# Experts of a hybrid block: the down product as seven half-sized products in place of eight, with the weight sums and three of the low parts on GpSimd

## The chip, the cores and the metric

The kernel runs on one core of a Trainium2 chip. The metric is the device time of one execution in microseconds. Each 32-bit product is made of three TensorE passes in a reduced format (fp32r): a value is split into a high part (a rounded copy) and a low part (value minus high part), and low·high, high·low and high·high are added up in PSUM.

## The reference

The block is a hybrid mixer (RWKV-7 and gated linear attention), a short convolution mixer, and a mixture of experts at the end. Only the last is touched:

```
def expert_choice_ffn(h, w_router, w_gate, w_up, w_down):
    aff = softmax(h @ w_router)                          # 2048 tokens, 16 experts
    g, idx = top_k(swapaxes(aff, 1, 2), cap)             # cap = 256 tokens per expert
    xs = h[idx]                                          # [16, 256, 1024]
    hid = silu(einsum('becd,edf->becf', xs, w_gate)) * einsum('becd,edf->becf', xs, w_up)
    ys = einsum('becf,efd->becd', hid, w_down) * g[..., None]
    return scatter_add(ys, idx)                          # [2048, 1024]
```

Each of the three weight matrices of an expert is 1024x1024 in float32 (4 MB), so an expert reads 12 MB.

## The kernel before, in words

Everything before the last stage is left as it is. The last stage (`experts`, with `choose` and `Choice`) loops over the 16 experts; each engine runs its own in-order program and they meet through counting semaphores.

- **Weights.** An expert's weights come in 12 pieces of 128x2048 (1 MB): pieces 0 to 7 are alternately gate and up (256 output columns each), 8 to 11 are two blocks of 128 rows of the down matrix each. SyncE loads a piece into one of four buffers (`w_loaded`) as soon as the low part of the piece four back is made (`load`, L2873). ScalarE makes the high part (`split_hi`, L2885), VectorE the low part (`split_lo`, L2889), each in a ring of six buffers.
- **Gate and up, f = 0 to 7.** For each of eight blocks of 128 hidden columns TensorE makes 24 gate and 24 up matmuls of 256 columns. ScalarE takes silu, VectorE multiplies (`hidden`), ScalarE makes its high part and VectorE its low part. f may start only when the `hidden` of f - 2 is made. After each odd f two more pieces are split. Beside f = 0 to 3 VectorE also marks the next expert's tokens (`mark`, 16 instructions), and before the `hidden` of f = 4 it reads their list out of PSUM (`keep`); GpSimd waits for that, and then gathers them by two indirect DMAs.
- **Turn.** 16 transposes of the gathered tokens of the next expert, once the `hidden` of f = 6 and 7 are made; ScalarE and VectorE make `x_hi`, `x_lo` (four instructions each).
- **Down.** 8 blocks of hidden rows x 2 halves of the tokens x 2 halves of the columns x 3 passes = 96 matmuls of 512 columns, into banks 4 to 7. Beside it ScalarE and VectorE split four pieces of the next expert.
- **End.** Four VectorE instructions scale the result (L3123), and GpSimd adds it to the output by two indirect DMAs.

GpSimd does no arithmetic on large tiles in this stage; in the first stage it does (L1150).

Of the kernel before, what the change touches and what calls it, by code (L numbers as in the profile page):

```python
# [14 lines left out]
F32 = mybir.dt.float32  # L15
# [2819 lines left out]
def experts(nc, k, wg, wu, wd, aff, idx_all, gate_all, out):  # L2835
# [8 lines left out]
    CH, LOADED, SPLIT, W = 12, 4, 6, KD * 256  # L2844
    F32R = mybir.dt.float32r
    with Phase("ex") as ctx:
        s = semaphores(nc, ctx, ["row", "load0", "load1", "load2", "load3", "hi", "lo", "used", "turned", "x_hi", "x_lo", "gu", "silu",
                                 "hid", "hid_hi", "hid_lo", "y", "ys", "idx", "gates", "consts", "parts", "at", "now", "hot", "listed", "chosen", "gate", "first"])
# [3 lines left out]
        raw = sb(nc, ctx, "w_loaded", [P, LOADED, W])  # L2852
        w_hi = [sb(nc, ctx, f"w_hi{i}", [P, W], F32R) for i in range(SPLIT)]
# [4 lines left out]
        h_hi = sb(nc, ctx, "hid_hi", [P, KD, CAP], F32R)  # L2858
        h_lo = sb(nc, ctx, "hid_lo", [P, KD, CAP], F32R)
        sl = sb(nc, ctx, "silu", [P, 2, CAP])  # L2860
        hid = sb(nc, ctx, "hidden", [P, 2, CAP])
# [8 lines left out]
        made = Choice(nc, ctx, k, s, idx_all, gate_all)  # L2870

        def load(sp, e, c):

            views = (gv, uv) if c < CH else (gv[1:], uv[1:])
            c = c % CH
            dst = raw[:, c % LOADED, :]
            if c < 8:
                src = views[c % 2][e, :, :, (c // 2) * 256:(c // 2 + 1) * 256]
                dst = dst.rearrange("p (kb f) -> p kb f", f=256)
            else:  # L2880
                dst = dst.rearrange("p (kb d) -> p kb d", d=D)
                src = dv[:, bass.ds(e * KD + (c - 8) * 2, 2), :]
            sp.dma_start(dst, src).then_inc(loads[c % LOADED], 16)

        def split_hi(act, e, c):  # L2885
            act.wait_ge(loads[c % LOADED], e * 48 + 16 * (c // LOADED + 1))
            nc.scalar.activation(w_hi[c % SPLIT][:], raw[:, c % LOADED, :], ACT.Copy).then_inc(s["hi"], 1)  # L2887

        def split_lo(dve, e, c):  # L2889
            dve.wait_ge(s["hi"], e * CH + c + 1)  # L2890
            nc.vector.tensor_tensor(w_lo[c % SPLIT][:], raw[:, c % LOADED, :], w_hi[c % SPLIT][:].bitcast(F32), ALU.subtract).then_inc(s["lo"], 1)  # L2891

        def passes(psum, lh, ll, rh, rl, first, last):

            nc.tensor.matmul(psum, ll, rh, start=first, stop=False)  # L2895
            nc.tensor.matmul(psum, lh, rl, start=False, stop=False)  # L2896
            return nc.tensor.matmul(psum, lh, rh, start=False, stop=last)  # L2897
# [31 lines left out]
        choose(nc, k, aff, made, xg, sl, Beside())  # L2929
        with nc.Block() as block:  # L2930
            @block.sync
            def _(sp):
                def turn(e, last, c0=0):
                    for c in range(c0, CH - LOADED if last else CH):
                        sp.wait_ge(s["lo"], e * CH + c + 1)
                        load(sp, e, c + LOADED)
                turn(0, False)
                with sp.Fori(1, NE - 1) as e:
# [4 lines left out]
            def _(pool):  # L2943
# [14 lines left out]
                def scatter(e, copied):  # L2958
# [8 lines left out]
                    for h in range(2):  # L2967
                        pool.wait_ge(sent[h], e * 16 + 16)
                gather(0, 1)
                pool.wait_ge(s["idx"], 2)  # L2970
                nc.gpsimd.tensor_tensor(mark[:], k.ident[:, 0:1], k.ident[:, 0:1], ALU.mult).then_inc(s["first"], 1)
                pool.wait_ge(s["first"], 1)
                with pool.Fori(0, NE - 1) as e:
                    for h in range(2):
                        pool.wait_ge(gathered[h], e * 16 + 16)
                    pool.wait_ge(s["turned"], e * 4 + 4)
                    gather(e + 1, e * 4 + 3)
                    scatter(e, e * 4 + 5)
                scatter(NE - 1, NE * 4 - 1)

            @block.tensor
            def _(pe):
# [8 lines left out]
                def turn(e, last):  # L2991
                    pe.wait_ge(s["x_lo"], e * 4 + 4)
                    for f in range(KD):
# [6 lines left out]
                        for half in range(2):  # L3000
                            c = 2 * q + half
                            if f % 2 == 0:
                                pe.wait_ge(s["lo"], e * CH + c + 1)
# [13 lines left out]
                    for f in range(KD):  # L3017
                        c = 8 + f // 2
                        pe.wait_ge(s["hid_lo"], e * KD + f + 1)
                        if f % 2 == 0:  # L3020
                            pe.wait_ge(s["lo"], e * CH + c + 1)
                        for h in range(2):
                            hs = slice(h * P, (h + 1) * P)
                            for b in range(2):
                                o = (f % 2) * D + b * 512
                                mm = passes(bank[4 + 2 * h + b][:], h_hi[:, f, hs], h_lo[:, f, hs], w_hi[c % SPLIT][:, o:o + 512],
                                            w_lo[c % SPLIT][:, o:o + 512], f == 0, f == KD - 1)
                        if f % 2:
                            mm.then_inc(s["y"], 1)
# [5 lines left out]
            def _(act):  # L3035
# [217 lines left out]
```

## Time and profile before

| what | us |
|---|---|
| median of 3 runs (lowest, highest) | 3490.54 (3489.82, 3493.35) |
| profiled execution: time | 3489.02 |
| profiled execution: span | 3487.2 |
| TensorE matmuls busy | 3289.8 |
| VectorE busy | 2187.5 |
| ScalarE busy | 1461.8 |
| GpSimd busy | 563.4 |

Busy times are sums over an engine's instructions. In timelines a row may merge several like instructions (xN); its time then runs from the first one's start to the last one's end. One instruction alone lasts a little longer than the distance at which the next can follow. The experts take the span from about 2330 us on.

### The profile page before, as it was taken

To read this page: it belongs to the slowest core of one execution; us is meant where nothing else is said; L and a number is where in the kernel's file an instruction comes from. 1 tells how busy PE (TensorE), PEld (TensorE's weight loads), DVE (VectorE), ACT (ScalarE), POOL (GpSimd) and SP (SyncE) were. 2 spreads that over 40 slices of the span, in tenths; PEclk is the share of its full clock that TensorE was granted. 3 is DMA by queue.
4 is the path that set the end of the run, shared out by engine and by line. 5 is a ranking of instruction groups with operands and counts; after the bars stand their busy time and mean duration, and the time that the engine had idled before them with its cause. 6 is when DMAs were issued, how large, how long until landed. Compare 5 with 4: busy or idle time off the path is not lost. (4 is left out here: it accounts for less than half of the span.)

```text
span 3487.2 us, 75240 instructions
## 1 busy us (share of the span) xinstructions
PE 3289.8 (94%) x31246; PEld 2817.5 (81%) x31246; DVE 2187.5 (63%) x3703; ACT 1461.8 (42%) x2121; POOL 563.4 (16%) x792
## 2 busy tenths in 40 slices
PE   7999999999699998989989999959999999999997
PEld 5778878788577886867877878749999999999997
DVE  4666766667554655677787866676555656565563
ACT  5445444444255665332233224424444444444442
POOL 3555555555100000000000000000100110011000
PEclk9999999999999999989999999959999999999999
DMA  4221222211233434422122244446666666666662
GB/s 146 57 83 52 66 75 61 80 51 51 67 127 109 142 113 156 134 85 68 65 73 85 77 157 157 148 137 203 214 209 207 212 205 206 214 199 215 200 217 73
DMA packets 361839, 452.83 MB, mean 130 GB/s; under 512 B 15189, under 2 KB 300149, under 8 KB 361589
## 3 DMA queue, kind: packets, MB, share of 16 engines
q1 hardware_dynamic: 350200, 407.33, 36.0%
q0 software_dynamic: 9216, 33.56, 4.1%
q10 hardware_dynamic: 2176, 8.39, 0.6%
q8 instruction: 188, 3.08, 0.4%
q14 instruction: 59, 0.48, 0.0%
HBM read 382.10 MB, written 67.13 MB: 129 GB/s over the span
## 5 line engine op out<-in xcount | busy, mean ns | idle before, releaser
L2895 PE MATMUL bank<-ex_x_hi,ex_w_lo 128*128 128x256 f32 x2048 | 581.4, 284 | 2.0 <-DVE ex_x_lo L3077 2.0
L2896 PE MATMUL bank<-ex_x_lo,ex_w_hi 128*128 128x256 f32 x2048 | 580.2, 283 | 0.0
L2897 PE MATMUL bank<-ex_x_hi,ex_w_hi 128*128 128x256 f32 x2048 | 580.1, 283 | 0.0
L2891 DVE TENSOR_TENSOR ex_w_lo<-ex_w_loaded,ex_w_hi 128x2048 fp32r<-128x2048 f32 x192 | 433.8, 2289 | 226.7 <-ACT ex_w_hi L2887 222.3
L2887 ACT ACTIVATE ex_w_hi<-ex_w_loaded 128x2048 fp32r<-128x2048 f32 x192 | 359.4, 1904 | 171.7 <-PE bank L2897 169.3
L2895 PEld LDWEIGHTS bank<-ex_x_hi,ex_w_lo 128*128 128x128 f32 x2048 | 393.6, 192 | 2.8 <-issue 2.2
L2896 PEld LDWEIGHTS bank<-ex_x_lo,ex_w_hi 128*128 128x128 f32 x2048 | 393.6, 192 | 0.6
L2897 PEld LDWEIGHTS bank<-ex_x_hi,ex_w_hi 128*128 128x128 f32 x2048 | 393.7, 192 | 0.0
L2338 PE MATMUL bank<-sc_tokens_hi,sc_w_lo 128*128 128x512 f32 x672 | 266.9, 397 | 28.6 <-DVE hidden_hT_split L2468 12.5
L2951 POOL CAST ex_idx<-kept_masks 128x2 uint32 (+1 forms) x16 | 3.0, 186 | 1735.7 <-POOLq L79 1424.7
L2340 PE MATMUL bank<-sc_tokens_hi,sc_w_hi 128*128 128x512 f32 x672 | 264.6, 394 | 0.0
L264 PE MATMUL bank<-columns_columns_hi,weights_weights_lo 128*128 128x512 f32 x544 | 226.6, 417 | 9.9 <-DVE columns_columns_lo L849 4.4
L3051 ACT ACTIVATE ex_hid_hi<-ex_hidden 128x256 fp32r<-128x256 f32 x128 | 53.4, 417 | 415.8 <-DVE ex_hidden L3100 415.8
L760 ACT ACTIVATE rw_E<-bank 128x256 f32<-128x256 f32 x160 | 61.0, 381 | 377.2 <-PE bank L371 377.2
L266 PE MATMUL bank<-columns_columns_hi,weights_weights_hi 128*128 128x512 f32 x544 | 214.0, 393 | 0.0
L265 PE MATMUL bank<-columns_columns_lo,weights_weights_hi 128*128 128x512 f32 x544 | 213.8, 393 | 0.0
L2895 PE MATMUL bank<-ex_w_hi,ex_hid_lo 128*128 128x512 f32 x512 | 200.8, 392 | 0.0
L2897 PE MATMUL bank<-ex_w_hi,ex_hid_hi 128*128 128x512 f32 x512 | 199.4, 390 | 0.0
L2896 PE MATMUL bank<-ex_w_lo,ex_hid_hi 128*128 128x512 f32 x512 | 199.2, 389 | 0.0
L1150 POOL TENSOR_TENSOR weights_weights_lo<-plain_weights,weights_weights_hi 128x1024 fp32r<-128x1024 f32 x67 | 164.1, 2450 | 205.8 <-ACT weights_weights_hi L614 205.6
L2338 PEld LDWEIGHTS bank<-sc_tokens_hi,sc_w_lo 128*128 128x128 f32 x672 | 128.2, 191 | 61.1 <-DVE hidden_hT_split L2468 14.3
L3100 DVE TENSOR_TENSOR ex_hidden<-ex_silu,bank 128x256 f32<-128x256 f32 x128 | 53.5, 418 | 157.1 <-PE bank L2897 157.1
(498 smaller groups left out, 8303.2 us busy)
## 6 DMA issues: line engine op xcount, KB each, us to landing
ex_w_loaded<-in_wg SPq DMA_DIRECT2D x64, 1024.0 KB, 5.4
ex_w_loaded<-in_wu SPq DMA_DIRECT2D x64, 1024.0 KB, 6.2
ex_w_loaded<-in_wd SPq DMA_DIRECT2D x64, 1024.0 KB, 5.1
plain_weights<-in_w_in SPq DMA_DIRECT2D x70, 512.0 KB, 4.7
gl_ada_tile<-in_ada_w SPq DMA_DIRECT2D x48, 512.0 KB, 4.4
plain_first_w<-in_sc_w_in SPq DMA_DIRECT2D x24, 1024.0 KB, 5.2
plain_columns<-hT_dram SPq DMA_DIRECT2D x14, 1024.0 KB, 7.5
plain_columns<-in_x SPq DMA_DIRECT2D x16, 512.0 KB, 5.7
```

The source lines that it names most:

```text
L264: nc.tensor.matmul(psum, lo[:, kb, :], h_hi[:, :, at], start=(kb == 0), stop=False)
L265: nc.tensor.matmul(psum, hi[:, kb, :], h_lo[:, :, at], start=False, stop=False)
L266: mm = nc.tensor.matmul(psum, hi[:, kb, :], h_hi[:, :, at], start=False, stop=(kb == KD - 1))
L760: nc.scalar.activation(eb[:], k.psum[:].rearrange("p (i x) -> p i x", x=512)[:, 4:6, 256:384].rearrange("p i (j t) -> p i j t", t=C), ACT. ...
L1150: nc.gpsimd.tensor_tensor(w_lo[n % 3], wraw[n % 3], w_hi[n % 3].bitcast(F32), ALU.subtract).then_inc(s["w_lo"], 1)
L2338: nc.tensor.matmul(psum, w_lo[:, at, kb, :], hi[:, kb, :], start=(kb == 0 and not more), stop=False, skip_group_check=more)
L2340: mm = nc.tensor.matmul(psum, w_hi[:, at, kb, :], hi[:, kb, :], start=False, stop=(kb == H - 1), skip_group_check=more)
L2887: nc.scalar.activation(w_hi[c % SPLIT][:], raw[:, c % LOADED, :], ACT.Copy).then_inc(s["hi"], 1)
L2891: nc.vector.tensor_tensor(w_lo[c % SPLIT][:], raw[:, c % LOADED, :], w_hi[c % SPLIT][:].bitcast(F32), ALU.subtract).then_inc(s["lo"], 1)
L2895: nc.tensor.matmul(psum, ll, rh, start=first, stop=False)
L2896: nc.tensor.matmul(psum, lh, rl, start=False, stop=False)
L2897: return nc.tensor.matmul(psum, lh, rh, start=False, stop=last)
```

## The change

The down product `hid @ w_down` of an expert is cut into 2x2 blocks on each side: A11, A12, A21, A22 are `hidden` by halves of the tokens and of the hidden rows (stored turned), B11 to B22 the down matrix by halves of its rows and columns. Seven products replace eight (Winograd's form):

- S3 = A11 - A21, S2 = A22 - S3, S1 = A21 + A22, S4 = A12 - S2, made on VectorE; T1 = B12 - B11, T2 = B22 - T1, T3 = T2 - B11, T4 = B21 - T2, made on GpSimd (`block_sum`).
- The products, in the order in which TensorE makes them, are A11·B11, S3·T3, S1·T1, S2·T2, A12·B21, A22·T4, S4·B22: below P0 to P6. Each is 4 x 3 matmuls of 512 columns, 84 in all. P4, P5 and P6 go on adding in the banks of P0, P1 and P2.
- VectorE adds the banks up: `middle` 1 is u2 = P0 + P3, 2 is v2 = u2 + P1, 3 is v2 + P2. P5 may start only after `middle` 2 and P6 after `middle` 3, as they write the same banks.

There are now 15 pieces to split per expert (8, and B11, T3, T1, T2, B21, T4, B22 as numbers 8 to 14) in rings of five. The low parts of pieces 0, 1 and B21 are made on GpSimd, the other 12 on VectorE. The high and low parts of the hidden blocks are made in 7 instructions of 512 columns each, in place of 8 of 256 each. The down matrix is loaded by blocks: no bytes are added. The core of the diff:

```diff
-    CH, LOADED, SPLIT, W = 12, 4, 6, KD * 256
+    CH, LOADED, PIECES, SPLIT, W, H = 12, 4, 15, 5, KD * 256, KD // 2
+    B11, T3, T1, T2, B21, T4, B22 = range(8, 15)
+    POOL_LO = (0, 1, B21)
...
+                def block_sum(e, c):
+                    n = SUMS.index(c)
+                    for slot in {T1: (0, 1), T2: (2,), T3: (), T4: (3,)}[c]:
+                        pool.wait_ge(loads[slot], e * 48 + 48)
...
+                    if c == T3:
+                        lo_made(pool, e, B11)
...
+                    nc.gpsimd.tensor_tensor(raw_of(c), one, other, ALU.subtract).then_inc(s["t"], 1)
...
+                def turn(e, last):          # GpSimd
+                    block_sum(e, T1)
+                    block_sum(e, T2)
+                    if not last:
...
+                        gather(e + 1, e * 4 + 3)
+                    block_sum(e, T3)
+                    block_sum(e, T4)
+                    split_lo(pool, nc.gpsimd, e, B21, s["lo_pool"])
+                    if not last:
+                        split_lo(pool, nc.gpsimd, e + 1, 0, s["lo_pool"])
+                        split_lo(pool, nc.gpsimd, e + 1, 1, s["lo_pool"])
...
+                    for n, a in enumerate(A_ORDER):          # TensorE
+                        c, more = B11 + n, n >= 4
+                        pe.wait_ge(s["a_lo"], e * 7 + LO_ORDER.index(a) + 1)
+                        lo_made(pe, e, c)
+                        if a == A12:
+                            pe.wait_ge(s["p1"], e + 1)
+                        if a in (A22, S4):
+                            pe.wait_ge(s["middle"], e * 3 + (2 if a == A22 else 3))
+                        for kb in range(H):
...
                     for f in range(KD):                      # ScalarE
...
+                        if f == 3:
+                            hidden_hi(e, A11)
+                            hidden_hi(e, S3)
+                        if f == 7:
+                            hidden_hi(e, S1)
                         if f % 2:
+                            act.wait_ge(s["gu"], e * 2 * KD + 2 * f + 2)
+                            split_hi(act, e, f + 4)
+                            if f == 7:
+                                hidden_hi(e, S2)
+                                hidden_hi(e, A12)
+                            split_hi(act, e, f + 5)
+                    hidden_hi(e, A22)
+                    act.wait_ge(s["y"], e * 7 + 1)
+                    act.wait_ge(s["idx"], e * 4 + 3)
+                    nc.scalar.activation(u2, bank[4][:], ACT.Copy).then_inc(s["p1"], 1)
+                    split_hi(act, e, T4)
+                    hidden_hi(e, S4)
                     if not last:
...                                                           # the four x_hi
+                    act.wait_ge(s["y"], e * 7 + 2)
+                    split_hi(act, e, B22)
+                    if not last:
+                        for d in range(SPLIT):
+                            act.wait_ge(s["y"], e * 7 + d + 3)
+                            split_hi(act, e + 1, d)
...
+                        if f == 3:                           # VectorE
+                            hidden_sum(e, S3)
+                            hidden_lo(e, A11)
+                        if f % 2 and f < 7:
+                            lo(f + 4)
+                            lo(f + 5)
+                    hidden_sum(e, S2)
+                    hidden_sum(e, S1)
+                    hidden_lo(e, S3)
+                    hidden_lo(e, S1)
+                    hidden_sum(e, S4)
+                    hidden_lo(e, S2)
+                    lo(T2)
+                    hidden_lo(e, A12)
+                    hidden_lo(e, A22)
+                    lo(T4)
+                    hidden_lo(e, S4)
+                    lo(B22)
+                    nc.vector.tensor_copy(gates[:], gav[...]).then_inc(s["gates"], 1)
...
+                    nc.vector.tensor_tensor(u2, u2, bank[5][:], ALU.add).then_inc(s["middle"], 1)
...
+                    nc.vector.tensor_tensor(v2, u2, bank[6][:], ALU.add).then_inc(s["middle"], 1)
...
+                    nc.vector.tensor_tensor(v2, v2, bank[7][:], ALU.add).then_inc(s["middle"], 1)
...
+                    scaled(1, 1, v2)
...                                                           # x_lo, two more sums, three more scaled
+                    if not last:
+                        for d in range(2, SPLIT):
+                            split_lo(dve, nc.vector, e + 1, d, s["lo"])
```

## Rows read from the trace of the kernel before

**Rows 1.** Windows, stage and one cycle: length; busy (xinstructions) PE, PEld, DVE, ACT, POOL; clock; DMA share, GB/s.
```profile
2330.00:3470.00 1140.00, 1135.29 (x8432) 1071.95 (x8432) 670.37 (x891) 490.05 (x523) 96.42 (x126) 1.00 0.64 202
...
2766.00:2836.50 70.50, 70.50 (x530) 66.67 (x529) 42.21 (x57) 31.15 (x33) 6.13 (x8) 1.00 0.66 208
```

**Rows 2.** Timeline, VectorE: start us, us, engine, line, what. `keep` of two experts in turn.
```profile
2443.80 0.16 DVE L2822 TENSOR_REDUCE kept_masks<-bank 128x4 f32 x1
...
2514.31 0.15 DVE L2822 TENSOR_REDUCE kept_masks<-bank 128x4 f32 x1
```

**Rows 3.** Timeline, TensorE: gate and up, turn, down, and the next expert's first matmul.
```profile
2812.76 0.28 PE L2897 MATMUL bank<-ex_x_hi,ex_w_hi 128*128 128x256 f32 x1
2812.89 1.91 PE L2906 MATMUL bank<-kept_masks,ex_x_gathered 128*128 128x128 f32 x16
2814.55 0.47 PE L2895 MATMUL bank<-ex_w_hi,ex_hid_lo 128*128 128x512 f32 x1
...
2836.21 0.39 PE L2897 MATMUL bank<-ex_w_hi,ex_hid_hi 128*128 128x512 f32 x1
2836.44 0.28 PE L2895 MATMUL bank<-ex_x_hi,ex_w_lo 128*128 128x256 f32 x1
```

**Rows 4.** Timeline, ScalarE: two high parts in a row, one alone, four of 512 columns.
```profile
2813.96 3.70 ACT L2887 ACTIVATE ex_w_hi<-ex_w_loaded 128x2048 fp32r<-128x2048 f32 x2
2817.56 2.04 ACT L3037 ACTIVATE ex_x_hi<-bank 128x512 fp32r<-128x512 f32 x4
2820.32 1.92 ACT L2887 ACTIVATE ex_w_hi<-ex_w_loaded 128x2048 fp32r<-128x2048 f32 x1 [0.72 <-PE bank L2897]
```

**Rows 5.** Timeline, VectorE, beside Rows 4 and the end of the down product.
```profile
2813.17 0.42 DVE L3100 TENSOR_TENSOR ex_hidden<-ex_silu,bank 128x256 f32<-128x256 f32 x1 [3.07 <-PE bank L2897]
...
2815.89 4.49 DVE L2891 TENSOR_TENSOR ex_w_lo<-ex_w_loaded,ex_w_hi 128x2048 fp32r<-128x2048 f32 x2 [1.38 <-ACT ex_w_hi L2887]
2820.30 2.48 DVE L3077 TENSOR_TENSOR ex_x_lo<-bank,ex_x_hi 128x512 fp32r<-128x512 f32 x4
...
2841.17 2.73 DVE L3123 SCALAR_TENSOR_TENSOR ex_y<-bank,ex_gates,ex_g_row 128x512 f32<-128x512 f32 x4 [0.21 <-DVE ex_gates L3116]
```

**Rows 6.** Groups, GpSimd, whole span: count, busy us, mean ns, idle before.
```profile
L1150 POOL TENSOR_TENSOR weights_weights_lo<-plain_weights,weights_weights_hi 128x1024 fp32r<-128x1024 f32 x67 | 164.1, 2450 | 205.8 <-ACT weights_weights_hi L614 205.6
L1155 POOL TENSOR_TENSOR rw_tanh_g_or_cs_before<-rw_cs,rw_sw 128x512 f32<-128x512 f32 x16 | 20.6, 1284 | 90.8 <-DVE rw_cs L881 90.8
```

**Rows 7.** Timelines, first stage: VectorE with both inputs in SBUF beside GpSimd.
```profile
133.19 3.27 DVE L849 TENSOR_TENSOR columns_columns_lo<-plain_columns,columns_columns_hi 128x1024 fp32r<-128x1024 f32 x1
...
132.57 2.81 POOL L1150 TENSOR_TENSOR weights_weights_lo<-plain_weights,weights_weights_hi 128x1024 fp32r<-128x1024 f32 x1
135.33 1.40 POOL L1161 TENSOR_TENSOR rw_nt<-rw_scores,mixers_masks 128x128 f32<-128x128 f32 x1
```

**Rows 8.** Timelines, first stage: VectorE with an input in PSUM beside GpSimd.
```profile
17.73 0.69 DVE L840 TENSOR_TENSOR plain_columns<-bank,rw_norm_cols 128x512 f32<-128x512 f32 x1 [0.42 <-PE bank L247]
...
16.99 2.35 POOL L1150 TENSOR_TENSOR weights_weights_lo<-plain_weights,weights_weights_hi 128x1024 fp32r<-128x1024 f32 x1 [16.53 <-ACT weights_weights_hi L614]
```

**Rows 9.** By line, VectorE: ns min/median/max of 16, first and last start.
```profile
L849 DVE TENSOR_TENSOR columns_columns_lo<-plain_columns,columns_columns_hi x16: 1217/1320/3273, 19.4 to 652.7; 128x1024 fp32r<-128x1024 f32 x16
L888 DVE TENSOR_SCALAR rw_a<-rw_a,rw_derived x16: 545/2472/2481, 54.6 to 839.6; 128x512 f32<-128x512 f32 x16
```

**Rows 10.** Transfers in window 2780 to 2851: count, KB each, median us to landing.
```profile
ex_w_loaded<-in_wd SPq DMA_DIRECT2D x4, 1024.0 KB, 5.3
...
ex_w_loaded<-in_wu SPq DMA_DIRECT2D x4, 1024.0 KB, 5.6
```

**Rows 11.** Timeline, GpSimd: the gather of the next expert's tokens.
```profile
2796.69 0.18 POOL L2951 CAST ex_idx<-kept_masks 128x2 uint32 x1 [19.34 <-DVE kept_masks L2822]
...
2799.02 0.96 POOL L2955 DMA_INDIRECT ex_x_gathered<-h_dram,ex_idx  x1 [0.30 <-issue]
```

More of the change, by code:

```diff
@@ L2843, in experts @@
     dv = wd.rearrange("o e (kb p) d -> p (o e kb) d", p=P)
-    CH, LOADED, SPLIT, W = 12, 4, 6, KD * 256
+    CH, LOADED, PIECES, SPLIT, W, H = 12, 4, 15, 5, KD * 256, KD // 2
     F32R = mybir.dt.float32r
+    B11, T3, T1, T2, B21, T4, B22 = range(8, 15)
+    A11, S3, S1, S2, A12, A22, S4 = range(7)
+    SUMS = (T1, T2, T3, T4)
+    LOAD_OF = {B11: 8, B22: 10, B21: 11}
+    BLOCK = {8: (0, 0), 9: (0, 1), 10: (1, 1), 11: (1, 0)}
+    BANK_OF = (4, 6, 7, 5, 4, 6, 7)
+    POOL_LO = (0, 1, B21)
+    DVE_LO = tuple(c for c in range(PIECES) if c not in POOL_LO)
+    POOL_STEP = CH // len(POOL_LO)
+    A_ORDER = (A11, S3, S1, S2, A12, A22, S4)
+    LO_ORDER = (A11, S3, S1, S2, A12, A22, S4)
+    HI_SLOT = (0, 1, 2, 3, 4, 5, 0)
     with Phase("ex") as ctx:
-        s = semaphores(nc, ctx, ["row", "load0", "load1", "load2", "load3", "hi", "lo", "used", "turned", "x_hi", "x_lo", "gu", "silu",
-                                 "hid", "hid_hi", "hid_lo", "y", "ys", "idx", "gates", "consts", "parts", "at", "now", "hot", "listed", "chosen", "gate", "first"])
+        s = semaphores(nc, ctx, ["row", "load0", "load1", "load2", "load3", "hi", "lo", "lo_pool", "t", "turned", "x_hi", "x_lo", "gu", "silu",
+                                 "hid", "a_sum", "a_hi", "a_lo", "y", "p1", "middle", "sum", "ys", "idx", "gates", "consts", "parts", "at", "now", "hot", "listed", "chosen", "gate", "first"])
         gathered = [ctx.enter_context(nc.semaphore(f"gathered{h}")) for h in range(2)]
@@ L2932, in _ @@
             def _(sp):
-                def turn(e, last, c0=0):
-                    for c in range(c0, CH - LOADED if last else CH):
-                        sp.wait_ge(s["lo"], e * CH + c + 1)
+                def turn(e, last):
+                    for c in range(4):
+                        lo_made(sp, e, c)
                         load(sp, e, c + LOADED)
-                turn(0, False)
-                with sp.Fori(1, NE - 1) as e:
+                    for c in range(4):
+                        lo_made(sp, e, 4 + c)
+                        load(sp, e, 8 + c)
+                    if not last:
+                        for c, used in enumerate((T3, T1, B22, B21)):
+                            lo_made(sp, e, used)
+                            load(sp, e, CH + c)
+                with sp.Fori(0, NE - 1) as e:
                     turn(e, False)
```

170 lines of the change are left out of this document (103 added, 67 removed).

## The prediction

> **What bounds the kernel now.** I read the windows first. In the experts' stage TensorE is busy 1135 of 1140 us at a granted clock of 1.00 (2.4 GHz) and in one expert's cycle all 70.50 us; VectorE has 42 of these 70.5, ScalarE 31, GpSimd 6, the DMA engines a share of 0.66 [rows 1]. The timeline of `keep` gives the cycle between experts: 2514.31 - 2443.80 = 70.51 us [rows 2]. The reader should see that nothing but TensorE sets this stage, so a product less is worth its full length only if TensorE still never waits. TensorE's timeline cuts the cycle: gate and up 46.9 us (2766.0 to 2812.9), turn 1.7, down 2836.44 - 2814.55 = 21.9 for 96 matmuls, 0.228 each [rows 3].
>
> **The product less.** 84 matmuls in place of 96: 12 x 0.228 = 2.7 us per expert, 16 x 2.7 = 43.8 us in all. The cycle with no wait is 70.5 - 2.7 = 67.8. The whole question is what TensorE waits for in it.
>
> **Durations of what is added.** ScalarE's high part of a piece: 1.8 us from start to start (two take 3.70, one 1.92), 0.5 for 512 columns [rows 4]. VectorE's low part: 2.2 (two take 4.49, less 2.29 for one), 0.6 for 512 columns [rows 5]. GpSimd subtracting 2048 columns isn't in the trace; 1024 columns take 2.35 to 2.45 and 512 take 1.28 [rows 6, 8], so 1.07 more per 512, and 2.35 + 2.14 = 4.5. The ends are 4.0 (less than twice 2.35, if the fixed part is large) and 4.9 (twice 2.45); I take 4.5. GpSimd has seven per expert, 31.5 us, beside 6 now: by sums it has room. VectorE does 12 pieces as before (the three more are GpSimd's), 4 block sums (2.4), 7 low parts of 512 columns (4.3, for 8 of 256 before), 5 bank sums (3.1). ScalarE gets three more pieces, 5.4. By sums every engine fits into 67.8. DMA bytes are the same.
>
> **What the sums hide.** In the first stage GpSimd does such subtractions, and there VectorE and GpSimd shut each other out. L849 on VectorE, both inputs in SBUF, takes 1.22 us alone; begun at 133.19 beside a GpSimd instruction that ran 132.57 to 135.38 it took 3.27 and ended at 136.46, 1.1 us behind the other's end; and GpSimd's next, begun at 135.33, took 1.40 and ended just behind L849 [rows 7, 9]. So one waits for the other's whole instruction, and they take turns. L888, with a single SBUF input, takes 0.55 alone and 2.47 in most of its 16 [rows 9]. An addition with one input in PSUM isn't touched: L840 took 0.69 wholly inside GpSimd's 16.99 to 19.34 [rows 8]. In the experts, VectorE's low parts of pieces and hidden blocks, its four block sums and three of four final scalings have both inputs in SBUF: 12 x 2.2 + 2.4 + 4.3 + 1.8 = 34.9 us. With GpSimd's 31.5 that is 66.4 us of 67.8 that exclude each other. Before, GpSimd had none. The bounds for this cost: nothing, if every exclusion falls into idle time (cycle 67.8), up to the timetable below at its worst.
>
> The Trainium skill (SBUF — State Buffer, Who interferes with whom) states the same in general: a VectorE instruction with two SBUF inputs and a GpSimd instruction that reads SBUF hold a shared port for the whole instruction. It adds that VectorE copies from SBUF to SBUF can be shut out as well; of that the last rival speaks. By the sums of busy time alone the change gives its 43.8 us; by this rule, which the rows bear out, it does not.
>
> **The timetable, gate and up.** I follow one cycle with 0 at its first gate matmul; block f ends at 5.8, 11.5, 17.3, 23.0, 29.8, 35.5, 41.2, 46.9. At 0 VectorE still owes two scalings (to 3.4) and the low parts of pieces 2, 3, 4 (to 10.0): with rings of five they can't be made sooner. Piece 5 is split behind f = 1: high 13.4, low 15.6; its buffer then takes B12, and a load lands 5.4 us later [rows 10], at 21.0. GpSimd makes T1 21.0 to 25.5. VectorE wants S3 at 23.4 and gets it 25.5 to 26.1; GpSimd T2 26.1 to 30.6; VectorE the low part of A11 to 31.2, piece 7 to 33.4, B11 to 35.6, then `keep`, 35.8, and the `hidden` of f = 4, 36.2. f = 6 is held for it 0.8 us; f = 7 ends at 47.7. `keep` releases the gather, 3.3 us [rows 11], to 39.1, and only behind it come T3 (43.6) and T4 (48.1). ScalarE stands at the high part of T3 from 35.9 on: T3 45.4, T1 47.2. VectorE's low part of T3 is shut out by T4 until 48.1: 50.3; T1 52.5; and behind these two in its program is the `hidden` of f = 6: 52.9. The turn needs it at 47.7. **First wait: 5.2 us.**
>
> **The timetable, down.** Now 0 is that 52.9. VectorE: `hidden` 0.4, S2 and S1 1.8, low parts of S3 and S1 3.0, S4 3.7. ScalarE is one unbroken chain: S1 2.3, T2 4.1, S2 4.7, A12 5.2, B21 7.0, A22 7.5, copy of P0 8.0, T4 9.8, S4 10.3, four `x_hi` 12.2, B22 14.0, next piece 0 15.9, piece 1 17.7. VectorE: S2 5.3, T2 7.5. GpSimd, asking since 7.0, has B21 from 7.5 to 12.0. VectorE: A12 and A22 13.2, T4 15.4, S4 16.0. TensorE: turn 2.0, P0 4.7, P1 7.5, P2 10.2, P3 12.9, P4 15.7. P5 needs `middle` 2, and VectorE's program has the low part of B22 ahead of that. At 15.9 GpSimd asks for piece 0, at 16.0 VectorE for B22. GpSimd first: B22 20.5 to 22.7, `middle` 2 at 24.3; VectorE first: B22 18.2, `middle` 2 at 19.8. P5 waits 8.6 or 4.1 us; the two askings are 0.1 apart, so I take the mean, 6.4. **Second wait: 6.4 us.** The scaling ahead of `x_lo` is then shut out by GpSimd's next piece, which holds the next f = 0 by 0.5, and f = 2 waits some 0.5 for a `hidden` behind the late low parts: with the 0.8 above, 1.8 us of small waits.
>
> **Sum.** 67.8 + 5.2 + 6.4 + 1.8 = 81.2 us per cycle, 10.7 more than 70.5. Fifteen cycles: 160.5. The last expert has no gather and no next pieces: -2.7 and waits of 2 to 5, +1. The profiled execution took 3489.0 us (span 3487.2 and 1.8 around it); 3489.0 + 161.5 = 3650.5. The median of the runs, 3490.5, is 1.5 above the profiled execution: **3652 us**.
>
> The ring of five instead of six costs nothing beyond what stands in this table. The marking beside f = 0 to 3 is taken as not shut out; no GpSimd tile is in work there.
>
> **Rivals.**
> 1. *One of the two large waits falls away*, as its asking comes in a luckier order (a load or `keep` a few us sooner lets T1 to T4 pass before f = 7). For it: each wait hangs on in-order chains with slips of 2 us. Against it: at 66.4 of 67.8 us a slip is only moved. First wait alone: 67.8 + 7.0 = 74.8, 16 x 4.3 = 69, 3559; second alone: 8.2 - 2.7 = 5.5, 88, 3578. Range 3495 to 3605.
> 2. *Nothing is shut out.* Then ScalarE's chain decides: B22 is high at 14.0, low at 16.2, `middle` 2 at 17.9, where P5 could start at 15.7. That wait of 2.2 eats most of the 2.7: cycle 70.0 to 70.5, 3483 to 3491. Against it are [rows 7, 9].
> 3. *Faster: the sums are right.* GpSimd's subtractions fall into VectorE's waits for ScalarE and TensorE (28 of 70.5 us idle [rows 1]), B22 and the banks' sums come in time, TensorE never waits: 16 x 2.7, 3447. It decides once the waits per expert are below 2.7. For it: every engine has room by its sum. Against it: 66.4 us of exclusion.
> 4. *A copy is shut out too.* The copy of the gates, 2 elements from SBUF to SBUF, stands between B22 and `middle`, and is like L888 in having one SBUF input [rows 9]; if it waits for GpSimd's piece 1 (22.7 to 27.2), `middle` 2 is at 28.8 and P5 waits 13.1: cycle 87.9, 15 x 17.4 + 1 = 262, 3752. The page's rule named above speaks for this; no row shows so small a copy beside GpSimd's large tiles.
>
> **Chances and range.** Forecast (3605 to 3710) 0.48; rival 1, 0.20; rival 2, 0.08; rival 3 or a part of it, 0.13; rival 4, 0.09; something above that, 0.02. Of 2 in 10 to leave out I leave most of rival 3 below and what is above 3740: range 3484 to 3740, the likeliest case's own 3605 to 3710. A change of 0.2% (7 us) is about what a measurement of this kernel tells from none. Faster takes rival 3 and the lower edge of rival 2: 0.15; same 0.07; slower 0.78.
>
> **What would show it.** In the changed profile: VectorE's low parts of 2048 columns with a median near 2.3 but a maximum of 6 to 7 us, GpSimd's near 4.5 with some at 6.7; TensorE idle ahead of the transposes, released by `hidden` (5 us), and ahead of P5, released by VectorE's bank sum (4 to 9 us); a distance between `keep` instructions near 81. TensorE busy throughout with a distance of 67.8 would prove the table wrong; if GpSimd's instructions take 4.5 and VectorE's low parts never exceed 2.3, the exclusion is the wrong step; if they do and TensorE still doesn't wait, the order in time is.

## The result and the profile after

| | before | changed kernel |
|---|---|---|
| median of 4 runs (lowest, highest), us | 3490.71 (3489.82, 3493.35) | 3771.81 (3771.12, 3775.06) |
| profiled span, us | 3487.2 | 3773.2 |
| mean cycle of an expert in the loop, us | 70.51 | 88.42 |

The ratio is 1.0806, with a 95% interval of 1.0787 to 1.0824: slower by 281 us, where 161 (3652 us) were forecast. The direction was right; the time lies 32 us above the range. The mean cycle is read from the register instruction ahead of `keep` (L2822), which every pass of the loop has once: (last start - first) / 14.

The windows of the experts' stage (as [rows 1]: busy us of TensorE, its weight loads, VectorE, ScalarE, GpSimd, then granted clock, DMA share, GB/s):

```profile
2330.00:3750.00 1420.00, 1193.45 (x8223) 1107.04 (x8224) 1113.74 (x1017) 598.41 (x571) 723.38 (x236) 0.90 0.51 162
```

TensorE is busy 84% of the stage, not 99.6%, and the granted clock is 0.90, not 1.00. What TensorE waited for (total us, times, longest):

```profile
PE bank L2924 <- DVE ex_y L3246: 112.0, 16, 8.2
PE bank L2924 <- DVE plain_ex_hidden L3221: 54.8, 16, 4.4
PE bank L2935 <- DVE plain_ex_hidden L3221: 53.1, 15, 5.1
```

In this order: P5 for `middle` 2, 7.0 us each; f = 6 for `hidden` of f = 4, 3.4; the turn for `hidden` of f = 6 and 7, 3.5. They are three waits of the forecast (6.4, 0.8, 5.2): 13.9 us a cycle against 12.4, or 13.4 with the two small waits of 0.5 us that did not come.

The groups behind them (those answering to [rows 5 to 7]; busy us, mean ns | idle before):

```profile
L2920 DVE TENSOR_TENSOR ex_w_lo<-ex_w_loaded,ex_w_hi 128x2048 fp32r<-128x2048 f32 x162 | 499.8, 3125 | 191.4 <-ACT ex_w_hi L2916 186.9 <-POOL ex_mark L3043 4.5
L2920 POOL TENSOR_TENSOR ex_w_lo<-ex_w_loaded,ex_w_hi 128x2048 fp32r<-128x2048 f32 x46 | 245.8, 5356 | 251.2 <-ACT ex_w_hi L2916 251.2
L3203 DVE TENSOR_TENSOR ex_hid_lo<-plain_ex_hidden,ex_hid_hi 128x512 fp32r<-128x512 f32 x64 | 140.4, 2212 | 1.5
L3240 DVE COPY ex_gates<-kept_masks 128x2 f32 x15 | 66.8, 4454 | 0.0
```

The low part of a piece, 2.29 us before, has a mean of 3.1 (median 2.28, longest 6.71), that of a hidden block 2.2 instead of 0.69, and the copy of the gates, two columns, 4.45 us instead of 0.16. Ahead of P5, VectorE's timeline and under it GpSimd's:

```profile
2856.86 2.28 DVE L2920 TENSOR_TENSOR ex_w_lo<-ex_w_loaded,ex_w_hi 128x2048 fp32r<-128x2048 f32 x1
2859.06 4.45 DVE L3240 COPY ex_gates<-kept_masks 128x2 f32 x1
2863.55 0.69 DVE L3244 TENSOR_TENSOR ex_y<-ex_y,bank 128x512 f32<-128x512 f32 x1
2864.27 0.69 DVE L3246 TENSOR_TENSOR ex_y<-ex_y,bank 128x512 f32<-128x512 f32 x1
```

```profile
2856.89 11.12 POOL L2920 TENSOR_TENSOR ex_w_lo<-ex_w_loaded,ex_w_hi 128x2048 fp32r<-128x2048 f32 x2 [3.91 <-ACT ex_w_hi L2916]
```

B22's low part and GpSimd's piece 0 are asked for within 0.03 us. B22 gets through, GpSimd has its turn next, and the copy waits for it: 2859.06 to 2863.51. `middle` 1 and 2 follow, and P5 starts at 2865.01, its first matmuls 0.43 us apart:

```profile
2865.01 0.79 PE L2924 MATMUL bank<-ex_w_hi,ex_hid_lo 128*128 128x512 f32 x1 [6.83 <-DVE ex_y L3246]
2865.60 0.63 PE L2925 MATMUL bank<-ex_w_lo,ex_hid_hi 128*128 128x512 f32 x1
2866.03 0.63 PE L2926 MATMUL bank<-ex_w_hi,ex_hid_hi 128*128 128x512 f32 x1
...
2871.37 0.40 PE L2924 MATMUL bank<-ex_w_hi,ex_hid_sums_lo 128*128 128x512 f32 x1
2871.61 0.40 PE L2925 MATMUL bank<-ex_w_lo,ex_hid_hi 128*128 128x512 f32 x1
```

0.43 against 0.235 further on is the lower of TensorE's two levels (1.2 against 2.4 GHz). The windows beside it show the granted clock:

```profile
2860.00:2865.00 5.00, 0.00 (x0) 0.00 (x0) 4.90 (x4) 0.10 (x1) 5.00 (x2) 0.59 0.95 298
2865.00:2870.00 5.00, 4.99 (x12) 3.93 (x13) 4.96 (x5) 1.81 (x1) 3.60 (x2) 0.50 1.08 347
2870.00:2875.00 5.00, 5.00 (x27) 4.26 (x26) 3.58 (x6) 3.16 (x2) 0.00 (x0) 0.89 0.61 194
```

The same happens behind the waits of f = 6 and of the turn. In one cycle (2912.74 to 3001.02) I summed what the slow matmuls of 512 and 256 columns lie further apart than at full clock (0.233 and 0.12): 38 of them, 5.06 us, called "half-clock excess" in the expectations below. That cycle is not a typical one: its 16 transposes ran at full clock, in 1.7 us, where in 12 of the 14 cycles of the loop they took 3.1 to 3.2. So the account below is the mean of all 14 cycles. At full clock with no wait the matmuls of a cycle take 68.3 us: 45.9 gate and up and 1.6 transposes as before, 19.7 for the 84 down matmuls at 0.234, 1.1 for the marking and the joints. TensorE's account of a cycle is thus 88.4 = 13.9 of waits + 68.3 + 6.2 over. Of the 6.2 some 0.26 belong to each wait even where the clock stays up (experiment 2), and about 5.4 are half clock.

The block sums: GpSimd and VectorE in the next gate and up part.

```profile
2899.45 4.63 POOL L3039 TENSOR_TENSOR ex_w_loaded<-ex_w_loaded 128x2048 f32<-128x2048 f32 x1 [15.60 <-DMA ex_w_loaded<-in_wd]
2904.25 6.42 POOL L3039 TENSOR_TENSOR ex_w_sums<-ex_w_loaded 128x2048 f32<-128x2048 f32 x1 [0.17 <-POOL ex_w_loaded L3039]
...
2916.24 4.59 POOL L3039 TENSOR_TENSOR ex_w_loaded<-ex_w_sums,ex_w_loaded 128x2048 f32<-128x2048 f32 x1
2920.98 4.64 POOL L3039 TENSOR_TENSOR ex_w_sums<-ex_w_loaded,ex_w_sums 128x2048 f32<-128x2048 f32 x1
```

```profile
2900.45 12.36 DVE L2920 TENSOR_TENSOR ex_w_lo<-ex_w_loaded,ex_w_hi 128x2048 fp32r<-128x2048 f32 x2 [1.84 <-ACT ex_w_hi L2916]
2912.74 0.15 DVE L2822 TENSOR_REDUCE kept_masks<-bank 128x4 f32 x1
...
2922.82 7.15 DVE L2920 TENSOR_TENSOR ex_w_lo<-ex_w_loaded,ex_w_hi 128x2048 fp32r<-128x2048 f32 x2 [9.20 <-ACT ex_w_hi L2916]
2929.90 0.74 DVE L3221 TENSOR_TENSOR plain_ex_hidden<-ex_silu,bank 128x256 f32<-128x256 f32 x2
```

Two low parts take 12.36 us instead of 4.5 beside T1 and T2, two take 7.15 beside T4. T1 starts 26.0 us after f = 0 (2873.48), not 21.0; over the 15 cycles it is 24.2 to 26.0, with a median of 24.7, so this cycle is a late one. The median landing of a down block over the whole run is now 8.5 us where it was 5.1 (5.3 in the window of [rows 10]).

### The profile page after: what moved, and what is told of

Same layout as the page of the kernel before. It is cut to its first block and busy times, and to the rows that moved or that the text cites. A ratio compares the mean times of both kernels' runs of the same rounds, so it can differ in the third digit from the quotient of the medians.

```text
span 3773.2 us, 75797 instructions
## 1 busy us (share of the span) xinstructions
PE 3356.3 (89%) x31054; PEld 2859.1 (76%) x31054; DVE 2632.1 (70%) x3833; ACT 1569.9 (42%) x2169; POOL 1189.8 (32%) x902
## 5 line engine op out<-in xcount | busy, mean ns | idle before, releaser
L2924 PE MATMUL bank<-ex_x_hi,ex_w_lo 128*128 128x256 f32 x2048 | 596.6, 291 | 56.7 <-DVE plain_ex_hidden L3221 54.8
L2920 DVE TENSOR_TENSOR ex_w_lo<-ex_w_loaded,ex_w_hi 128x2048 fp32r<-128x2048 f32 x162 | 499.8, 3125 | 191.4 <-ACT ex_w_hi L2916 186.9
L2925 PE MATMUL bank<-ex_x_lo,ex_w_hi 128*128 128x256 f32 x2048 | 591.5, 289 | 0.0
L2926 PE MATMUL bank<-ex_x_hi,ex_w_hi 128*128 128x256 f32 x2048 | 590.9, 289 | 0.0
L2916 ACT ACTIVATE ex_w_hi<-ex_w_loaded 128x2048 fp32r<-128x2048 f32 x208 | 389.0, 1913 | 422.4 <-POOL ex_w_loaded L3039 199.6
L2924 PEld LDWEIGHTS bank<-ex_x_hi,ex_w_lo 128*128 128x128 f32 x2048 | 404.8, 198 | 60.8 <-DVE ex_w_lo L2920 53.8
L2925 PEld LDWEIGHTS bank<-ex_x_lo,ex_w_hi 128*128 128x128 f32 x2048 | 405.3, 198 | 0.6
L2920 POOL TENSOR_TENSOR ex_w_lo<-ex_w_loaded,ex_w_hi 128x2048 fp32r<-128x2048 f32 x46 | 245.8, 5356 | 251.2 <-ACT ex_w_hi L2916 251.2
L2338 PE MATMUL bank<-sc_tokens_hi,sc_w_lo 128*128 128x512 f32 x672 | 265.3, 395 | 27.3 <-DVE hidden_hT_split L2468 13.1
L2924 PE MATMUL bank<-ex_w_hi,ex_hid_lo 128*128 128x512 f32 x256 | 120.2, 470 | 114.5 <-DVE ex_y L3246 112.0
L2924 PEld LDWEIGHTS bank<-ex_w_hi,ex_hid_lo 128*128 128x128 f32 x256 | 56.5, 221 | 135.1 <-DVE ex_y L3246 113.2
```

The source lines that it names most:

```text
L2338: nc.tensor.matmul(psum, w_lo[:, at, kb, :], hi[:, kb, :], start=(kb == 0 and not more), stop=False, skip_group_check=more)
L2916: nc.scalar.activation(w_hi[c % SPLIT][:], raw_of(c), ACT.Copy).then_inc(s["hi"], 1)
L2920: on.tensor_tensor(w_lo[c % SPLIT][:], raw_of(c), w_hi[c % SPLIT][:].bitcast(F32), ALU.subtract).then_inc(signal, POOL_STEP if signal is s ...
L2924: nc.tensor.matmul(psum, ll, rh, start=first, stop=False, skip_group_check=more)
L2925: nc.tensor.matmul(psum, lh, rl, start=False, stop=False, skip_group_check=more)
```

## The experiments

Each was timed in three rounds beside the kernel before, the last in five. A time is followed by its ratio to before. Unless said otherwise they are edits of the changed kernel, whose cycle is 88.4 us and whose time 3771.8.

**1. The copy of the gates moved to the head of the cycle** (e_copy).

```diff
                 def turn(e, last):                       # VectorE
+                    dve.wait_ge(s["ys"], e * 2 + 1)
+                    nc.vector.tensor_copy(gates[:], gav[...]).then_inc(s["gates"], 1)
...
                     lo(B22)
-                    nc.vector.tensor_copy(gates[:], gav[...]).then_inc(s["gates"], 1)
```

> Only the copy of the gates moves, from between the low part of B22 and the banks' sums to the start of the cycle, where GpSimd has no large tile in work. Theory (exclusion, copy shut out for 4.45 us per expert right ahead of the sum that P5 waits for): P5's wait falls from 7.5 to about 3.5 us, 15 x 4.3 = 65 us less, 3707, and some us more if TensorE keeps its clock over the shorter wait. Rival (P5 is held by something else, the copy only fills a wait): 3772, no change.

3708.35 us, 1.0621 [1.0604, 1.0639], as expected: 64 less for an instruction of two columns. Cycle 83.9. P5's waits fall from 112.0 to 46.0:

```profile
PE bank L2924 <- DVE plain_ex_hidden L3223: 67.7, 19, 5.3
PE bank L2935 <- DVE plain_ex_hidden L3223: 48.9, 15, 5.1
PE bank L2924 <- DVE ex_y L3247: 46.0, 16, 3.8
```

**2. GpSimd's seven instructions on one column** (e_tiny): same order and signals, next to no time.

```diff
-            on.tensor_tensor(w_lo[...][:], raw_of(c), w_hi[...][:]...)
+            w = 1 if on is nc.gpsimd else W
+            on.tensor_tensor(w_lo[...][:, 0:w], raw_of(c)[:, 0:w], w_hi[...][:, 0:w]...)
...
-                    nc.gpsimd.tensor_tensor(raw_of(c), one, other, ALU.subtract)
+                    nc.gpsimd.tensor_tensor(raw_of(c)[:, 0:1], one[:, 0:1], other[:, 0:1], ALU.subtract)
```

> GpSimd's seven subtractions per expert work on one column in place of 2048 (so the block sums and three low parts are left out and the output is not the reference's); all waits and the order stay. Theory (exclusion and the 4.5 us of each are the whole loss; ScalarE's chain alone would make P5 wait 2.2 us): cycle about 70.5 to 71, 3490 to 3500. Rival (rings of five, the order of the programs or the longer chain of sums cost TensorE the time): above 3600.

3528.52, 1.0122 [1.0085, 1.0158]: of the 281 us, 243 go with GpSimd's columns, but 28 more stay than expected. Cycle 71.8. In the profiled execution (3518.46) 9 of the 29 us above before lie ahead of the experts: the first `keep` starts at 2337.7 and not at 2328.9. VectorE's low parts and its copy are back at their times from before, and one wait is left, P5's, 2.7 us each:

```profile
L2921 DVE TENSOR_TENSOR ex_w_lo<-ex_w_loaded,ex_w_hi 128x2048 fp32r<-128x2048 f32 x162 | 364.0, 2288 | 103.5 <-ACT ex_w_hi L2916 99.0 <-POOL ex_mark L3046 4.5
L3243 DVE COPY ex_gates<-kept_masks 128x2 f32 x15 | 2.4, 162 | 0.0
```

```profile
PE bank L2925 <- DVE ex_y L3249: 43.2, 16, 3.7
```

That wait is rival 2's: ScalarE's chain sets B22 (2.2 forecast). So in this order seven products gain nothing even with GpSimd free.

The wait is 2.63 us in each of the 14 cycles, but what follows it differs. In 8 cycles TensorE's time outside the wait is 68.6 us, 0.26 over the 68.3; in the other 6 it is 69.9 to 70.1. The windows behind P5's start, at 2415.88 in one of the 6 and at 2561.41 in one of the 8, show the granted clock:

```profile
2417.50:2419.50 2.00, 2.00 (x6) 1.52 (x6) 2.00 (x4) 0.00 (x0) 0.00 (x0) 0.50 1.09 370
2563.00:2565.00 2.00, 2.00 (x10) 1.60 (x9) 2.00 (x4) 0.00 (x0) 0.00 (x0) 1.00 1.09 371
```

**3. GpSimd writes but doesn't read** (e_memset): the seven subtractions as memsets of 2048 columns, 1.8 us each, behind a one-column operation.

```diff
-            on.tensor_tensor(w_lo[c % SPLIT][:], raw_of(c), ...)
+                nc.gpsimd.tensor_tensor(mark2[:], k.ident[:, 0:1], k.ident[:, 0:1], ALU.mult)...
+                on.memset(w_lo[c % SPLIT][:].bitcast(F32), 0.0)...
```

> GpSimd's seven subtractions per expert become a one-column instruction and a memset of the same 2048-column tile: it writes as much and reads nothing (block sums and three low parts left out). Theory (what is shared is a way of reading SBUF): no VectorE instruction is stretched though GpSimd is busy 2 us or more each time; about the time of the one-column kernel plus little, 3490 to 3520. Rival (any large GpSimd instruction shuts VectorE out): VectorE's maxima rise by the memset's length and the time lies well above that of the one-column kernel.

3564.44, 1.0216 [1.0199, 1.0233], 44 above the upper expectation. VectorE's low parts keep their 2288 ns, but the copy doesn't:

```profile
L2926 DVE TENSOR_TENSOR ex_w_lo<-ex_w_loaded,ex_w_hi 128x2048 fp32r<-128x2048 f32 x162 | 363.9, 2288 | 119.8 <-ACT ex_w_hi L2917 115.3 <-POOL ex_mark L3052 4.6
L3249 DVE COPY ex_gates<-kept_masks 128x2 f32 x15 | 28.4, 1895 | 0.0
```

In one cycle the copy runs 2931.67 to 2933.57 and a memset 2931.75 to 2933.55. So reading decides for subtractions with two SBUF inputs, and a copy is shut out by writing as well. The Trainium skill (SBUF — State Buffer, Who interferes with whom) makes the same difference: a VectorE instruction with two SBUF inputs contends with a GpSimd instruction that reads SBUF and not with one that only writes it, while a copy in a two-port mode contends with GpSimd. The 2288 ns and the 1895 ns agree.

P5's wait is 4.4 us here, and behind it TensorE's time outside the wait is 70.7 in the mean, 2.4 over the 68.3.

**4. TensorE kept at work ahead of f = 6** (e_fill).

```diff
+                        if f == 6 and not last:
+                            for n in range(14):
+                                nc.tensor.matmul(bank[7][:], x_hi[:, n % 8, 0:P], x_hi[:, 0:2, :], start=True, stop=True)
```

> 14 extra matmuls of 512 columns into a free bank (3.3 us) ahead of the block f = 6, where TensorE waits 3.6 us on average for hidden of f = 4. Theory (the granted clock falls to half behind a wait because TensorE stood idle; about 2.5 of the 5.1 us per cycle lost at half clock stand there): the wait shrinks by what the extra matmuls fill, the slow stretch behind it goes, 15 x 2.5 = 38 us less, 3735. Rival (the clock falls for another reason, as a limit on power): no gain, or up to 15 x 3.3 = 50 us more, 3772 to 3822.

3774.03, 1.0813 [1.0795, 1.0831]: nothing gained, a miss of 39 us. The wait of f = 6 went from 54.8 to 10.6 us in all and the turn's rose from 53.1 to 75.8: VectorE's chain (`keep`, gather, T3, T4, low parts of T3 and T1, `hidden`) decides when the turn starts, however fast TensorE gets there.

**5. TensorE kept at work ahead of P5** (e_fill5).

```diff
+                        if a == A22:
+                            for m in range(26):
+                                nc.tensor.matmul(bank[4][:], zero[:], w_hi[...][...], start=False, stop=False, skip_group_check=True)
```

> 26 matmuls of 512 columns with an all-zero stationary tile, added to the bank of P4 (it stays what it was), ahead of P5, where TensorE waits 7.5 us on average: 6.1 us of it are filled. Behind this wait 13 matmuls run at half the granted clock, 3.0 us, and from there to the block f = 3 TensorE itself sets the time. Theory (the fall of the clock behind the wait is real time here): 15 x 3.0 = 45 us less, 3727. Rival (as with the filled wait ahead of f = 6, which gained nothing, another engine sets the time): 3772.

3755.84, 1.0761 [1.0743, 1.0779]: 16 less, 29 short of what was expected. TensorE's time over the 68.3 (and over the 6.1 of the added matmuls) goes from 6.2 to 3.8 us in the mean cycle, P5's wait from 112.0 to 22.6 in all. Of the 2.4 us a cycle that the clock gave back, 1.1 arrived in the time.

**6. The down loads at half their bytes** (e_half).

```diff
+                dst = dst[:, 0:2]
+                src = (dv, dv[:, H:])[kh][:, bass.ds(e * KD, 2), b * 512:(b + 1) * 512]
```

> The four loads of the down matrix per expert move half their bytes (the other half of each tile stays as it was: that part of the down product is left out). In the changed kernel B12 lands 10 us after its issue, not 5.4, and GpSimd's T1 starts at 26.0 us of the cycle, not at 21. Theory (the late landing delays T1, T2, keep, gather, T3, T4 and with them hidden of f = 4 and 6): about 3.9 us less per cycle, 58 us less, 3714. Rival (the VectorE and GpSimd chain would be as late without it): no change, 3772.

3748.15, 1.0744 [1.0725, 1.0763]: 24 less, 34 short of what was expected. The expectation rested on the late cycle shown above (26.0). The median landing falls from 8.5 to 6.5 us, and T1 starts 22.8 us after f = 0 in the median cycle where it was 24.7: 1.9 us sooner. There it meets others of VectorE's instructions (0.69 us each when alone):

```profile
2885.88 3.57 DVE L3200 TENSOR_TENSOR plain_ex_hidden_sums<-plain_ex_hidden 128x512 f32<-128x512 f32 x1
2889.37 5.12 DVE L3204 TENSOR_TENSOR ex_hid_lo<-plain_ex_hidden,ex_hid_hi 128x512 fp32r<-128x512 f32 x1
```

**7. Another order on ScalarE and VectorE, GpSimd as it is** (e_order): the copy early, the high parts of T3 and T1 and their low parts further forward or back, `hidden` of f = 6 and 7 ahead of T3 and T1, banks' sums ahead of T4 and B22.

```diff
                     hidden_sum(e, S2)
+                    lo(T3)
...
-                    lo(T4)
-                    hidden_lo(e, S4)
-                    lo(B22)
...
+                    lo(T4)
+                    hidden_lo(e, S4)
+                    lo(B22)
```

> Same work, other order: copy of the gates at the start of the cycle; hidden of f = 4 ahead of the low part of B11; hidden of f = 6 and 7 ahead of the low parts of T3 and T1; the banks' sums ahead of the low parts of T4 and B22. Theory (VectorE and GpSimd exclude each other for 66 of 68 us, so a wait taken away in one place comes back in another, now ahead of P3 or P5): cycle 75 to 81, 3570 to 3660. Rival (the changed kernel's loss is a fault of its order alone): cycle at most 71, below 3500.

3773.72, 1.0815 [1.0797, 1.0833]: no gain, where at least 110 us were expected. TensorE's waits only changed their name:

```profile
PE bank L2924 <- DVE ex_w_lo L2920: 163.4, 62, 4.7
PE bank L2935 <- DVE plain_ex_hidden L3226: 32.9, 14, 2.4
```

B22's low part, now last, also frees the buffer of the next expert's piece 2, and ScalarE stands 15.95 us ahead of that piece's high part for its load.

**8. Only the three low parts on one column** (e_tiny_lo; the block sums whole).

```diff
+            w = 1 if on is nc.gpsimd else W          # in split_lo alone
```

> GpSimd's three low parts work on one column (so these parts are left out), its four block sums are whole. Theory: the first half of the cycle stays as it is (T1 to T4 hold hidden of f = 4 and 6), in the down product only ScalarE's chain is left, P5 waits 2.7 us as with all seven on one column, and the clock stays up there: cycle 79 to 81, 3620 to 3655. Rival (the low parts are what does the harm): cycle near 71, below 3520.

3651.14, 1.0467 [1.045, 1.0485]: the low parts are worth 121 us, the sums 123 more. Both parts that were given to GpSimd weigh the same, taken away in this order; the other order was not run.

**9. Edits 1, 5 and 6 together** (e_three), with ten zero matmuls in place of 26.

> The changed kernel with three single edits together: the copy of the gates at the start of the cycle, the four down loads of an expert at half their bytes (half of the down matrix's columns of each block is left as it was in the buffer, so the products are of other numbers), and ten matmuls with a zero stationary matrix ahead of the last down product (they add zero). Apart they gave 3708 (64 us less), 3748 (24 less) and 3756 (16 less) against 3772. Theory A, the three errors of the forecast are separate links of one cycle and add up: 3772 - 64 - 24 - 16 = 3668 us, range 3645 to 3690, cycle about 81.8 us, which is near the forecast's 81.2. Theory B, they are one slack counted three times (the last product waits for VectorE, and each edit only takes from this same wait): no better than the best of them less a few us, 3690 to 3710. Above 3710: an edit harms another. Half-clock excess: A 2 to 3 us a cycle, B 4 to 5.

3685.23, 1.0557 [1.0526, 1.0588]: 87 us less, where the three alone gave 104. The time lies inside the range of theory A (3645 to 3690), but its four executions reach 3690.9, where theory B begins; the cycle is 82.5 (81.8 by A), and TensorE's time over the 68.3 is 3.8 us, between the 2 to 3 of A and the 4 to 5 of B. So they look like mostly separate links, with some 17 us shared or lost by the shorter filling.

**10. All low parts and sums on VectorE** (e_dve).

```diff
-    POOL_LO = (0, 1, B21)
+    POOL_LO = ()
...
-                    nc.gpsimd.tensor_tensor(raw_of(c), one, other, ALU.subtract).then_inc(s["t"], 1)
+                    nc.vector.tensor_tensor(raw_of(c), one, other, ALU.subtract).then_inc(s["t"], 1)
...
                         if f == 3:                       # VectorE
+                            lo(7)
+                            block_sum(e, T1)
+                            lo(B11)
+                        if f == 4:
+                            block_sum(e, T2)
+                        if f == 5:
+                            block_sum(e, T3)
+                            block_sum(e, T4)
+                            lo(T3)
```

> The changed kernel with no elementwise work on GpSimd at all (it keeps the gather and the scatter): all fifteen low parts of a cycle and the four block sums on VectorE, the copy of the gates at the start of the cycle, the sums placed at f = 3, 4, 5 of the hidden loop. Nothing is left out. Theory A, the loss is the exclusion of VectorE by GpSimd's subtractions: VectorE then runs 7 x 2.29 us more than now less what it stands shut out, about 63 us busy in a cycle of 73 to 77 us, 3540 to 3600 us: faster than the changed kernel, slower than before. Rival B, seven products with their sums need more of VectorE than the cycle has, whichever engine shares: it can't follow and TensorE waits 10 us or more a cycle, 3650 us or more. Rival C, with GpSimd idle the seventh product's saving shows: under 3490 us.

3530.08, 1.011 [1.0086, 1.0133], 10 better than the range and as good as GpSimd's instructions at one column. Cycle 73.4. VectorE does all the work that was meant to be taken from it, and the kernel is 242 us faster for it: GpSimd's help cost more than its whole load on VectorE (7 x 2.2 = 15.4 us a cycle). The order of VectorE's and ScalarE's programs differs here as well; e_order, whose order is near to this one, gained nothing with GpSimd at work. Left are waits of 31.8 us (f = 0, for the next expert's first low part) and 18.4 us (f = 2).

**11. The same with its order mended at these two waits** (e_dve2).

```diff
                     for f in range(KD):                  # ScalarE
...
+                        if f == 0:
+                            split_hi(act, e, 4)          # and the low part likewise
...
-                        if f == 7:
-                            hidden_hi(e, S1)             # now behind the high part of T2
...
                     hidden_sum(e, S1)                    # VectorE
+                    hidden_sum(e, S4)
                     hidden_lo(e, S3)
                     hidden_lo(e, S1)
-                    hidden_sum(e, S4)
-                    hidden_lo(e, S2)
                     lo(T2)
+                    hidden_lo(e, S2)
...
-                    scaled(1, 1, v2)
...
                         split_lo(dve, nc.vector, e + 1, 0, s["lo"])
+                        scaled(1, 1, v2)
```

> The kernel with all low parts and sums on VectorE, with its order mended where its trace shows TensorE waiting (2.1 us at f = 0 for the next expert's first low part, 0.6 us at f = 2, and 1.7 us of half-clock matmuls behind them, in a cycle of 73.4 us): on ScalarE T2's high part goes ahead of S1's and piece 4 is split after the silu of f = 0; on VectorE the S4 sum goes up, T2's low part ahead of S2's, piece 4's low part and one of the four scalings behind what f = 0 and f = 2 wait for. Nothing is left out. Theory A, these two waits are all that stands between this form and the seven products' saving: cycle 69 to 70.5 us, 3465 to 3490 us, faster than before by up to 0.7%. Rival B, VectorE (66 us busy) only moves the wait to another place: cycle 72 us or more, 3510 us or more.

3480.95 against 3488.49 us, 0.9979 [0.9969, 0.9988]: faster than both kernels, if only by 7.5 us (0.2%). Cycle 70.0, clock 1.00, VectorE busy 90%:

```profile
2330.00:3450.00 1120.00, 1096.14 (x8210) 1026.48 (x8210) 1008.64 (x1121) 598.35 (x571) 240.17 (x126) 1.00 0.65 205
```

```profile
PE bank L2924 <- DVE ex_w_lo L2920: 9.4, 15, 0.7
PE bank L2924 <- DVE plain_ex_hidden L3215: 8.3, 14, 0.6
```

## Why the prediction was right in direction and short by 120 us

**What bounds, and the product less.** Right that TensorE without a wait set the kernel. The cycle with no wait was put at 67.8; e_dve2 has 70.0 - 1.2 of waits = 68.8. Of that, 0.5 stands beside its two waits: the distance of 1.01 below holds 0.62 of wait and 0.39 for one matmul (0.23 elsewhere), and the next is 0.23 where 0.12 is usual.

```profile
2903.33 0.40 PE L2926 MATMUL bank<-ex_w_hi,ex_hid_hi 128*128 128x512 f32 x1
2904.34 0.39 PE L2924 MATMUL bank<-ex_x_hi,ex_w_lo 128*128 128x256 f32 x1 [0.62 <-DVE ex_w_lo L2920]
2904.57 0.28 PE L2925 MATMUL bank<-ex_x_lo,ex_w_hi 128*128 128x256 f32 x1
```

Without them the cycle is 68.3, so dropping a product is worth 2.2 us and not 2.7: in this cycle the down part is (2903.33 - 2883.88) / 83 = 0.234 a matmul where before it was 0.228, 0.5 us in all. Why stays open. 0.5 x 16 = 8 us of the miss.

**The exclusion.** Right, in place and kind: e_tiny, e_memset and e_dve take it away in three ways and each gives back over 200 us. GpSimd's 2048 columns took 4.6 us alone (4.5 forecast). VectorE and GpSimd took turns as forecast (two low parts in 12.36, T2 at 6.42, the low part of T3 behind T4), though in another order at T1: as T1 came late, S3 and the low part of A11 went ahead of it. One thing the runs do not part: all three also take away the length of GpSimd's subtractions, and ScalarE stood 14.2 us ahead of T3's high part for T3. A GpSimd as slow that shuts nobody out was not run, so how the first wait divides between exclusion and that length is not shown. For the second wait e_copy shows it.

**The first wait and the small ones.** The timetable had 5.2 + 1.8; measured are 3.4 + 3.5. Near in sum (6.9 against 7.0), shifted: T1 came 3.7 us later than put down in the median cycle (5.0 in the one shown), since a load was taken to land 5.4 us after its issue. Why landings take 8.5 us now is not shown; that the new order releases several loads close together is a guess, and the prediction didn't weigh it. e_half takes a part of the delay away, 24 us. Waits for `x_lo` or at f = 2 are not among the three above.

**The second wait: here the prediction failed.** Its size looks right, 7.0 against 6.4, but by two errors against each other. The step has VectorE's program go from the low part of B22 straight to `middle`; the copy between them was left free. In the trace the order was the kind one (VectorE first, `middle` 2 at 19.8 by the table), and the copy's 4.45 us, with 0.5 by which the low part of B22 came later than put down, bring it to the 24.75 measured (2865.01 - 2840.26, the `hidden` of f = 6); the wait came out no longer than 6.8 because P4 ended at 17.9 and not at 15.7: the transposes, at half clock behind the turn's wait, took 3.2 us (2840.72 to 2843.93) in place of 1.7. The step itself gave 4.1 us for this order, and the mean with the other order, 6.4, came near by luck. Moved, it gives 64 us back, over half of the 120. The evidence was on the table as rival 4, with L888 in [rows 9] and what the Trainium skill (SBUF — State Buffer, Who interferes with whom) says of copies; it got 0.09. The reason given, that no row showed so small a copy, was wrong in kind: the copy of two columns paid what was left of the other engine's instruction, 4.45 us, so its own size said nothing.

**A term that was missing: the clock.** The sum prices a wait at its length, and puts at nothing what follows it. Behind these waits TensorE ran on at its lower level, about 5.4 us a cycle. By TensorE's account alone this is the largest item: 88.4 - 81.2 = 7.2 = 5.4 (clock) + 0.8 (beside the waits at full clock) + 0.5 (down matmuls) + 0.5 (waits). But e_fill5 shows how little of it is cause: 2.4 us of clock given back at P5 moved the time by 1.1 a cycle, and e_fill gained none, as VectorE's chain arrives when it does. By cause the miss is 64 (copy) + 24 (landings) + 16 (clock at P5), and e_three has 87 of these 104 in one kernel; with the 8 of the matmuls some 25 of the 120 are left over, not traced.

**The rivals.** Rival 4 was the nearest (3752), and right that the copy is shut out. Its number is luck in part: it had the copy wait for piece 1 and P5 for 13.1 us, where the copy waited for piece 0 and P5 for 7.0; the 6.1 too much stood in for the 6.2 that TensorE lost behind and beside its waits, which were missing in it too. Rival 2 proved right as to what is behind the exclusion: with it gone P5 waits 2.7 us (2.2 forecast), and nothing is gained. Rival 3, the 44 us, was never near: even the best form found has 7.5.

## What to carry to other kernels

Before work is moved to an engine with time to spare, list the instructions of both engines that shut each other out; here 15 us a cycle of work taken from VectorE made the cycle 15 us longer (88.4 against 73.4), and the busy shares showed none of it. In a chain of waits price every such instruction between the last long one and the signal, the smallest too, at the whole of the other engine's instruction, and add to each wait what TensorE loses behind it (here 2.4 us behind 4.4, and 0.3 or 1.6 to 1.8 behind 2.6). Read such losses over all cycles: one alone can be the odd one, as here. Then undo the suspected instruction alone: moving one line told more than any sum.

## What the runs showed of the hardware

- A copy of 128x2 from SBUF to SBUF on VectorE took 4.45 us beside a GpSimd subtraction and 1.90 us beside a memset that began 0.08 us behind it, against 0.16 alone.
- Subtractions of 2048 columns on VectorE with both inputs in SBUF keep 2.29 us beside GpSimd's memsets and take up to 6.7 us beside its subtractions.
- Behind waits of 6.8 us the granted clock stood at 0.50 for the next 5 us. Behind one and the same wait of 2.63 us in e_tiny it stood at 0.50 in 6 of 14 cycles, at a price of 1.4 to 1.6 us, and at 1.00 in the other 8.
- A wait cost some 0.26 us more than its length even where the clock stayed at 1.00 (e_dve2, and 8 cycles of e_tiny).
- The median landing of a down block was 5.1 us before, 8.5 in the changed kernel, 6.5 at half the bytes and 11.3 in e_dve2, where it made nothing wait. What sets it was not settled.
